# A hybrid decoder layer on one core: the RWKV part recast (inverse levels as an engine loop, chunk steps as a scan, group norm in two token parts)

## The reference, cut to what matters

```python
def step(s, inp):                      # s: (N, H, E_value, E_key)
    r_t, w_t, k_t, v_t, a_t, b_t = inp
    sa = jnp.einsum('nhvk,nhk->nhv', s, a_t)
    s = s * w_t[:, :, None, :] + sa[..., None] * b_t[:, :, None, :] + v_t[..., None] * k_t[:, :, None, :]
    return s, jnp.einsum('nhvk,nhk->nhv', s, r_t)
...
mu_y = jnp.mean(y, axis=-1, keepdims=True)
var_y = jnp.mean(jnp.square(y - mu_y), axis=-1, keepdims=True)
y = ((y - mu_y) * lax.rsqrt(var_y + RWKV_GN_EPS)).reshape(n, t, RWKV_W)
y = y * lp['rwkv_ln_w'] + lp['rwkv_ln_b']
y_rwkv = ((y + bonus.reshape(n, t, RWKV_W)) * g).astype(h.dtype)
```

## Time and profile before

| what | value |
|---|---|
| median of 3 runs | 2193.56 us (2188.53 to 2202.67) |
| profiled execution, its own time | 2205.53 us |
| its span in the profile | 2203.7 us |
| granted PE clock, mean | 0.975 |
| PE / DVE / ACT / POOL busy | 97% / 54% / 39% / 9% |

### The profile page before, as it was taken

The page is one execution under the profiler, slowest core; times in us unless marked ns, Lnnn a source line. Parts: engine busy times, 40 slices in busy tenths (PEclk is TensorE's granted clock), DMA queues, the critical chain, the costliest instruction groups (busy, mean ns, idle before and its releaser), DMA issues.

```text
span 2203.7 us, 46115 instructions
## 1 busy us (share of the span) xinstructions
PE 2126.8 (97%) x19116; PEld 2095.9 (95%) x19116; DVE 1191.8 (54%) x1232; ACT 857.5 (39%) x954; POOL 194.6 (9%) x158
## 2 busy tenths in 40 slices
PE   6999999999999999999987889999999999999997
PEld 5999999999999999999985779999999999999997
DVE  5555555555455454769766446555555555544442
ACT  4444444444344343443323114444444444433332
POOL 3000000000000010044104720100000000000000
PEclk9999999999999999999997859999999999999998
DMA  5555555555555556587850105655555555555552
GB/s 158 183 180 182 180 181 181 181 180 182 172 182 188 174 186 189 163 224 230 255 160 9 32 24 175 188 180 180 178 185 179 183 179 181 182 165 194 189 170 97
DMA packets 359032, 373.52 MB, mean 169 GB/s; under 512 B 13329, under 2 KB 351797, under 8 KB 358742
## 3 DMA queue, kind: packets, MB, share of 16 engines
q1 hardware_dynamic: 349280, 348.17, 49.7%
q0 software_dynamic: 5920, 17.48, 3.1%
q10 hardware_dynamic: 3742, 6.52, 0.9%
HBM read 366.82 MB, written 5.32 MB: 169 GB/s over the span
## 4 chain that ended last, share of the span: by engine, by line
PE 91%; DVE 5%; DMA 2%; ACT 1%; issue 1%; ACTq 0%; POOL 0%; SPq 0%; POOLq 0%; DVEq 0%
PE ps L305 28%; PE ps L307 28%; PE ps L306 28%; DMA raw<-in_w_in_dram 2%; DVE wL L292 1%; PE ps L1066 1%; PE ps L1394 1%; PE ps L1609 1%; PE ps L1582 1%; PE ps L1678 0%; DVE xL L339 0%; PE ps L1601 0%; ACT wH L286 0%; PE ps L1665 0%; PE ps L1760 0%
## 5 line engine op out<-in xcount | busy, mean ns | idle before, releaser
L292 DVE TENSOR_TENSOR wL<-raw,wH 128x1024 fp32r<-128x1024 f32 (+1 forms) x676 | 828.4, 1231 | 864.1 <-ACT wH L286 863.8
L286 ACT ACTIVATE wH<-raw 128x1024 fp32r<-128x1024 f32 (+1 forms) x676 | 699.9, 1037 | 1013.5 <-PE ps L307 948.2
L305 PE MATMUL ps<-xH,wH 128*128 128x264 f32 x3616 | 1031.8, 285 | 12.6 <-DVE wL L292 12.6
L307 PE MATMUL ps<-xH,wL 128*128 128x264 f32 x3616 | 1029.7, 285 | 0.0
L306 PE MATMUL ps<-xL,wH 128*128 128x264 f32 x3616 | 1029.5, 285 | 0.0
L305 PEld LDWEIGHTS ps<-xH,wH 128*128 128x128 f32 x3616 | 683.9, 189 | 14.6 <-issue 13.9
L307 PEld LDWEIGHTS ps<-xH,wL 128*128 128x128 f32 x3616 | 683.5, 189 | 0.0
L306 PEld LDWEIGHTS ps<-xL,wH 128*128 128x128 f32 x3616 | 683.0, 189 | 0.2
L305 PE MATMUL ps<-hH,wH 128*128 128x264 f32 x1408 | 402.4, 286 | 0.0
L307 PE MATMUL ps<-hH,wL 128*128 128x264 f32 x1408 | 401.4, 285 | 0.0
L306 PE MATMUL ps<-hL,wH 128*128 128x264 f32 x1408 | 401.3, 285 | 0.0
(11 more groups left out here) (331 smaller groups left out, 1219.2 us busy)
## 6 DMA issues: line engine op xcount, KB each, us to landing
raw<-in_ffn_w_gate_dram SPq DMA_DIRECT2D x176, 512.0 KB, 3.4
raw<-in_ffn_w_up_dram SPq DMA_DIRECT2D x176, 512.0 KB, 3.5
raw<-in_ffn_w_down_dram SPq DMA_DIRECT2D x128, 512.0 KB, 3.5
raw<-in_w_in_dram SPq DMA_DIRECT2D x100, 512.0 KB, 4.8
raw<-in_ffn_w_down_dram SPq DMA_DIRECT2D x64, 384.0 KB, 3.1
raw<-in_w_out_dram SPq DMA_DIRECT2D x32, 512.0 KB, 4.6
kb<-in_cache_swa_k_dram POOLq DMA_DIRECT2D x24, 256.0 KB, 6.5
vb<-in_cache_swa_v_dram ACTq DMA_DIRECT2D x24, 256.0 KB, 5.4
```

Source lines behind the costliest of these rows:

```text
L286: nc.scalar.activation(wH[:, k % RING, 0:nk, :], raw[:, k % RING, 0:nk, :], ACT.Copy).then_inc(S("head_made"), 1)
L292: nc.vector.tensor_tensor(wL[:, k % RING, 0:nk, :], raw[:, k % RING, 0:nk, :], wH[:, k % RING, 0:nk, :].bitcast(F32), ALU.subtract).then_i ...
L305: nc.tensor.matmul(out, wH[:, k % RING, q, cols], high, start=a, stop=False)
L307: last = nc.tensor.matmul(out, wL[:, k % RING, q, cols], high, start=False, stop=b)
```

## The change

- The five levels are an engine loop on PE (`pe.Fori`), with waits against a register. The other engines' lists stay unrolled. Z's layout changes so that two heads of one pair lie side by side, and X is no longer grown: at each level PE transposes Z (six 128x128 transposes a pair) and ACT copies the result to `Xq`. The grams of X are gone; Aak comes ahead of the levels, the reads (Arb, Ark) behind them.
- The chunk steps become a scan: U is solved for all chunks at once (`pe_solved`, with own values and turned aT as one 128-column right side), a transition matrix is made for chunks 1 to 3 (`pe_transition`), and the state goes from chunk to chunk by one product and one DVE operation (`pe_state`, `state`). Outputs come in two groups (`pe_outputs`). Keys are turned for both the b and the k operand at once (`pe_turn_keys`).
- Group norm has two token parts (0 to 127, 128 to 263). The gain is multiplied into the spreading matrix `hs` by GpSimd during the gates (with a table `lnwr` loaded for it), the bias is added to `bv` by ACT; the gating runs on DVE for both parts.
- Samples: GpSimd first makes the products for S.a and then for S.(w r), the output is put together from them and two dot products, and then the state is updated and written. ACT's four heads of the output projection stand behind both RWKV heads; DVE's four tails stand at its end.

The diff, cut to its core:

```diff
+        with pe.Fori(0, LEVELS) as lv:
+            for n in range(2):
+                pe.wait_ge(S("grams_out"), 2 * n + 2)
+                pe.wait_ge(S("z_level"), lv * 2 + (n + 1))
+                for i in range(RT):
+                    pair = Zq[n][:, 2 * i:2 * i + 2, :].rearrange("p b c -> p (b c)")
+                    last = nc.tensor.transpose(wide(slice(0, P), 4 + 2 * n, i), pair, ident)
+                last.then_inc(S("level_x"), 1)
+                for i, b, cp in every():
+                    last = nc.tensor.matmul(place(HALF[b], 2 * n + cp, i), Aq[n][HALF[cp], slot(b, i), :],
+                                            Zq[n][HALF[cp], 2 * i + b, :], start=True, stop=True)
+                last.then_inc(S("level_q"), 1)
+            for n in range(2):
+                pe.wait_ge(S("grams_out"), 4)
+                pe.wait_ge(S("level_q_out"), lv * 2 + (n + 1))
+                pe.wait_ge(S("level_x_out"), lv * 2 + (n + 1))
+                for i, b, cp in every():
+                    last = nc.tensor.matmul(place(HALF[cp], 2 * n + b, i), Xq[n][HALF[b], i, cp, :],
+                                            Qq[n][HALF[b], slot(cp, i), :], start=True, stop=True)
+                last.then_inc(S("level_z"), 1)
...
+    def pe_solved(pe, m, first):
+
         for i, b, cp in every():
+            R = HALF[cp]
+            rhs = side_by_side(R, FQ_AT[m] * H + slot(b, i), TOKA_AT[m] * H + 2 * i + b)
+            last = nc.tensor.matmul(wide(HALF[1 - cp], first, 2 * i + b), Zq[m][R, 2 * i + b, :], rhs,
+                                    start=True, stop=True)
+        last.then_inc(S("solved"), 1)
...
+    def pe_state(pe, n, bank):
+
+        for i, b in both():
+            h, out = 2 * i + b, place(HALF[b], bank, i)
+            last = nc.tensor.matmul(out, KB[n][:, h, :], UV[n][:, h, :], start=True, stop=n == 0)
+            if n:
+                last = nc.tensor.matmul(out, LR[HALF[b], n - 1, i, C:2 * C], states[n - 1][HALF[b], i, :],
+                                        start=False, stop=True)
+        last.then_inc(S("states_made"), 1)
...
     def pe_chunks(pe):
         pe_inverse(pe)
+        pe_own_values(pe, 0, 4)
+        pe_own_values(pe, 1, 6)
+        pe.wait_ge(S("z_level"), 11)
+        pe_reads(pe, 1, 0)
+        pe.wait_ge(S("z_level"), 12)
+        pe_turn_keys(pe, 1, 2)
+        pe.wait_ge(S("tokens_staged"), 8)
+        pe_solved(pe, 0, 4)
+        pe.wait_ge(S("tokens_staged"), 9)
+        pe_turn_keys(pe, 0, 2)
+        pe.wait_ge(S("grams_out"), 5)
+        pe.wait_ge(S("tokens_staged"), 10)
+        pe_solved(pe, 1, 0)
+        pe.wait_ge(S("solved_v"), 3)
+        pe.wait_ge(S("solved_a"), 3)
+        pe_transition(pe, 1, 4)
+        pe_state(pe, 0, 7)
...
```

DVE's new list behind the levels, where the place of the sample reduce is to be seen:

```diff
+        reads(0)
+        solved(0)
+        solved(1)
+        transition(1)
+        state(1)
+        dve.wait_ge(S("sample_parts"), 3)
+        v.tensor_reduce(smy[:], S2[:, :, 0:C // 2], AX.X, ALU.add).then_inc(S("sample_sums"), 1)
+        reads(1)
+        state(2)
```

GpSimd's new list:

```diff
+        step(g.tensor_tensor(S2[:], S1[:], key(0), ALU.mult))
+        halve()
+        g.tensor_tensor(ycat[:], sv[:, 2:4, :], sv[:, 4:5, :].broadcast_to([96, 2, C]), ALU.mult
+                        ).then_inc(S("sample_parts"), 1)
+        step(g.tensor_tensor(sv[:, 0, :], sv[:, 1, :], sv[:, 4, :], ALU.mult))
+        pool.wait_ge(S("sample_sums"), 1)
         step(g.tensor_tensor(S2[:], S1[:], key(0), ALU.mult))
         halve()
         step(g.tensor_tensor(S1[:], S1[:], key(1), ALU.mult))
-        pool.wait_ge(S("sample_sums"), 1)
+        pool.wait_ge(S("sample_sums"), 3)
+        for value, dot in ((smal[:, 0:C], smal[:, C:C + 1]), (sv[:, 5, :], smal[:, C + 1:C + 2])):
+            step(g.tensor_scalar(ycat[:, 0, :], value, dot, None, ALU.mult))
+            step(g.tensor_tensor(smy[:], smy[:], ycat[:, 0, :], ALU.add))
+        for a in range(2):
+            g.tensor_scalar(ycat[:, a, :], smy[:], cgat[:, 48 + a:49 + a], None, ALU.mult).then_inc(S("sample_y"), 1)
         step(g.tensor_tensor(S2[:], val(smal[:, 0:C]), key(2), ALU.mult))
         step(g.tensor_tensor(S1[:], S1[:], S2[:], ALU.add))
         step(g.tensor_tensor(S2[:], val(sv[:, 5, :]), key(3), ALU.mult))
         g.tensor_tensor(S1[:], S1[:], S2[:], ALU.add).then_inc(S("sample_state"), 1)
         pool.wait_ge(S("sample_state"), 1)
         pool.dma_start(o[9][0].rearrange("b h v k -> (b h) v k"), S1[:]).then_inc(S("sample_state_out"), 16)
-        step(g.tensor_tensor(S2[:], S1[:], key(4), ALU.mult))
-        halve()
         pool.wait_ge(S("sample_state_out"), 16)
```

More of the change, by code:

```diff
@@ L1527, in build @@
     HALF = (slice(0, C), slice(C, P))
[L1528 to L1535, removed]
+    ORDER = (1, 2, 3, 0)
     def mask(m, bits=False):
@@ new lines, in pe_turn_keys, with pe_reads @@
+    def pe_turn_keys(pe, n, first):
+        c = chunk(n)
+        for i in range(RT):
+            low, high = (bT, pkr) if n % 2 else (pkr, bT)
+            nc.tensor.transpose(wide(HALF[0], first, i), low[:, i, c], ident)
+            last = nc.tensor.matmul(wide(HALF[1], first, i), high[:, i, c], ident, start=True, stop=True)
+        last.then_inc(S("tokens_turned"), 1)
+    def pe_reads(pe, n, first):
+        c = chunk(n)
+        for i in range(RT):
+            for k in range(4):
+                b, own = k % 2, k // 2 ^ k % 2
+                last = nc.tensor.matmul(place(HALF[n % 2 if own else 1 - n % 2], first + b, i),
+                                        (pkr if own else bT)[HALF[b], i, c], pr[HALF[b], i, c], start=True, stop=True)
+        last.then_inc(S("grams_made"), 1)
@@ new lines, in pe_outputs @@
+    def pe_outputs(pe, m, first):
+        for n in (2 * m, 2 * m + 1):
+            for i, b in both():
+                h, k = 2 * i + b, i % 3 * P + n % 2 * C
+                out = ps[HALF[b], first + i // 3, k:k + C]
+                last = nc.tensor.matmul(out, UV[n][:, h, :], AR[n][:, slot(b, i), :], start=True, stop=n == 0)
+                if n:
+                    last = nc.tensor.matmul(out, states[n - 1][HALF[b], i, :], LR[HALF[b], n - 1, i, 0:C],
+                                            start=False, stop=True)
+        last.then_inc(S("outputs"), 1)
@@ new lines, in solved @@
+        def solved(m):
+            first = (6, 2)[m]
+            act.wait_ge(S("solved"), m + 1)
+            cp(threes(Wq[m][:, RT:H]), wide_half(slice(0, P), first, 2, 1), ACT.Copy).then_inc(S("solved_a"), 1)
+            for q in range(2):
+                R = HALF[1 - q]
+                cp(threes(UV[2 * m + q][:, RT:H], R), wide_half(R, first, 2, 0), ACT.Copy).then_inc(S("solved_a"), 1)
+        keys(0)
+        keys(1)
+        solved(0)
+        solved(1)
+        keys(2)
+        keys(3)
@@ new lines, in solved, with transition @@
+        def solved(m):
+            first = (4, 0)[m]
+            dve.wait_ge(S("solved"), m + 1)
+            v.tensor_copy(threes(Wq[m][:, 0:RT]), wide_half(slice(0, P), first, 2, 1)).then_inc(S("solved_v"), 1)
+            for q in range(2):
+                R = HALF[1 - q]
+                v.tensor_copy(threes(UV[2 * m + q][:, 0:RT], R), wide_half(R, first, 2, 0)).then_inc(S("solved_v"), 1)
+        def transition(n):
+            first = (4, 0, 4)[n - 1]
+            out = LR[:, n - 1].rearrange("p (g i) (w c) -> p g i w c", g=2, w=2)
+            dve.wait_ge(S("transitions"), n)
+            eye = cm[:, 0:1, :].unsqueeze(1).broadcast_to([P, 2, 3, C])
+            linked([v.tensor_tensor(out[:, :, :, 1, :], wide_half(slice(0, P), first, 2, 1), eye, ALU.add)], dve)
+            v.tensor_tensor(out[:, :, :, 0, :], wide_half(slice(0, P), first, 2, 0),
+                            pr[:, :, chunk(n)].rearrange("p (g i) c -> p g i c", g=2), ALU.add
+                            ).then_inc(S("transitions_out"), 1)
@@ L1958, in dve_chunks @@
+        reads(1)
+        state(2)
+        reads(2)
+        transition(2)
+        reads(3)
+        state(3)
+        transition(3)
+        dve_group_centre(dve, 0)
+        state(4)
         dve.wait_ge(S("sample_turned_y"), 1)
         v.tensor_copy(pvr[:, :, T:N].rearrange("p j b -> p b j"),
-                      ps[:, 6, 384:432].rearrange("p (b j) -> p b j", b=NB)).then_inc(S("sample_y_placed"), 1)
-        dve_group_centre(dve, 2)
-        for k in range(2):
-            tail(dve, CK, OUT, OUT_PER, 0, k)
```

532 lines of the change are left out of this document (208 added, 324 removed).

## The result

The changed kernel takes 2228.7 us (median of four runs, 2223.7 to 2230.4), the kernel before 2191.6 beside it: a ratio of 1.0156 [1.0116, 1.0196]. It is slower by 1.6%, where 2163 and "faster" were forecast, and the time lies above the range. The profiled execution took 2230.4 us, 24.9 more than that of before; the medians differ by 37, since the profiled execution of before was 12 above its median.

A forecast was written before the change was run, and what follows sets the result against it. TensorE matmuls bound the feed-forward blocks and projections, left alone; each changed stretch had another limit. The first pair's output products were to reach 1303.0 instead of 1333.3, 30.3 us off the median 2193.56, forecasting 2163 us, range 2150 to 2196.

The forecast's parts named there:

- Start: Grams before the levels: fewer operands awaited, last own gram finished about 1199.6 where the first level began 1199.8, gain 0.2.
- Levels: Five inverse levels: 5.0 us an iteration, plus 1.4 for first-pass code; PE leaves at 1225.7, not 1247.9, gain 22.
- Loop refetched: Rival: the levels' loop code is fetched every iteration, 11.1 us instead of 5.0, time 2194 or 2220; chance 0.09.
- Chunk steps: From the levels' end at 1225.7 through solving, state scan, outputs and sums, at full clock, ending at 1259.6.
- Two more 1.4: PE in the chunk steps: two more state products after the first state's 0.7 us, at 1.4 us each.
- so I take 1.0: Chunk steps: PE clock taken as full, because nearly all products now use both row halves.
- Tile shapes alternate: Rival: in states and outputs K=128 and K=64 pairs alternate, 0.17 for each of 144 switches, time 2178; chance 0.13.
- Clock falls: Rival: PE clock drops in the chunk steps, their 29.5 us of PE work doubles, gain 4, time 2189; chance 0.22.
- Turned keys: PE in the chunk steps: 18 records of 128 columns, 1.5 us a call at full clock.
- Group norm: Two-part group norm and gating behind the chunk steps: 20.6 us, to 1280.2, against 29.6 before.
- Sample part on GpSimd: GpSimd waits 9 us for DVE's reduce; its state write lands at 1287 and is last, first output product 1289.4.
- The anchor: Gain worked out from the profiled execution of 2205.5 us, 12 above the median, but taken off the median 2193.56.

The follow-up runs named there:

- x2: Changed kernel with each group's twelve 128-row own products first, then twelve 64-row carried ones, sum of the two left out: 2178.9 us, one run.
- x1: Changed kernel in the same order, but carried state and output products overwrite the own ones instead of adding to them: 2224.5 us, one run.
- x4: Changed kernel with own and carried products alternating two by two, sum of the two left out: 2185.6 us, one run.
- the quadrant versions: Changed kernel with each 128-row state and output product split into two 64-row ones in two banks, added by DVE; first such version 2181.2 us, ratio 0.9948.
- e7: Changed kernel with the turned keys' transposes made plain products with the identity, order kept: 2217.9 us, one run.
- q5: The first of the quadrant versions, with DVE's reduce of the samples' output sum moved up behind the first reads: 2177.1 us, ratio 0.9925.
- e4: Changed kernel with the turned keys grouped, six transposes and then six products, instead of alternating: 2218.6 us, ratio 1.0113.

## Why the prediction was wrong

*Start and Levels* held: the loop starts at 1199.2 for 1199.6. Its first iteration took 7.2 us because the clock was at 0.50 in it up to 1203.3, the others 5.4 for 5.0 (the last 5.1), PE left at 1227.8 for 1225.7. PE's first four groups of an iteration took 3.2 us for 2.9, and from there to the next turn it was 2.25 for 2.07. The 1.4 for code in the first pass hardly came: in x2, where the clock stood at 1.0, that pass took 5.6 (1198.19 to 1203.83). The rival *Loop refetched* falls: q8 has fewer packets, and no iteration waits for code. By the Trainium skill (Runtime: NRT & Kernel Launch, Instruction fetch mechanics) a taken branch out of the current window forces a fetch; here neither the packets nor the gaps show one for a loop of 408 instructions, and it was the unrolled form that waited for code.

*Chunk steps* is the step that failed, in two of its terms. "Two more 1.4" (1.4 each, by the sum of 19.8) and "outputs 4.9" priced the changes of shape at nothing, and "so I take 1.0" gave them the full clock. Measured: states 1 to 3 took 7.8, 9.6 and 7.7 us and the outputs 30.3. The price itself stood in the rival *Tile shapes alternate*: 0.17 for each of 144 switches. At the full clock it was right: x2 runs four records in 0.138 us (22 own in 0.89, 22 carried in 0.64), the changed kernel in 0.514, so 0.19 a change. Too low was its chance, and a row behind it was misread. The 0.15 after L1646 had been taken as a cost of one way only, since "the way back shows nothing lost". The trace of before shows the way back too: six L1414 records start at 1250.19, 0.109 apart, and L1678 comes 0.20 behind the last of them, 0.09 late, and so it does behind the last L1414 at 1244.83.

```profile
1250.94 1.61 PE L1678 MATMUL ps<-Fc,Zq 64*64 64x64 f32 x24
```

So both ways cost, and in a group where each product changes, every product pays. The Trainium skill (TensorEngine Tiling (Array Packing), Key Properties) says that changing the tiling mode drains the engine, without a number; x1 to x4 fit that and give a price, and no run shows the draining itself.

The two rivals were also priced as if only one could come true. *Clock falls* (2189) and *shapes* (2178) each fit the range; both came, and one brought the other. In x2, x4 and the quadrant versions the chunk steps keep 1.00; where every product changes shape, the granted clock drops to 0.50 at 1254.5, three microseconds into state 1. What each adds can be estimated: 144 products at 0.257 and chunk 0's twelve at 0.08 are 38.0 us, and x2's are 10.9, so 27 for the changes at the full clock; measured are 55.4, so 17 more for the half clock. Together 44.5. From the start of state 0 to ACT's `mixH` the changed kernel takes 95.0 us and x2 40.5; the ten left of that difference are the half clock on what lies between (the turned keys, 5.85 us a call for 3.55, the transitions, the sums). In the time 49.8 are left, mainly because x2 then waits 5.6 for the state's write.

*Turned keys* "1.5 each" were 3.55, a change of kind that no rival had. That e7 takes 1.5 is luck: the forecast had 18 records one after the other, e7 has 24, two side by side.

*Group norm* held in form: in q5, from the end of the first sums (1268.8) to the weight tail's end (1290.0) are 21.2 us for 20.6.

*Sample part on GpSimd* held too, with its end hidden: the wait was 13.4 for 9 and the write would have landed at 1293.3 for 1287, because DVE's reduce ended at 1250.7 for 1244.7: 2.1 of that came from the levels, 4.1 from two calls of turned keys. In x2 it is what ends last, with the first product at 1293.1 for the 1289.4 of the sum. So without the alternation the sum's 30.3 us would have been 26.6 by the profiled times (2205.5 - 2178.9).

*The anchor* failed as well. The gain was worked out from one execution of before and taken off the median, 12 us below it. The runs of before on record follow their mean granted clock: the seven at 0.974 to 0.976 took 2199.2 to 2208.2 us, those at 0.983 and above took 2185.8 to 2194.5, and the profiled one had 0.975. Between 1190 and 1362 its trace has 67 us at the half clock; outside that stretch all traces of this case have 38 to 50, and behind the fourth chunk of the output projection all have the same 870.2 to 870.4. So the 12 us lie most likely in the very stretch that the change replaces, and were counted twice; only one trace of before was kept, so this is inferred. By the profiled times the forecast is 2175.2. x2's 2178.9 is 16 above 2163: 3.7 from the sample part, 12 from this.

The signs listed were the right ones: "PEclk 0.50 in the chunk steps" and "state products above 2 us" both came.

## What to carry to other kernels

Before merging products of other shapes, or transposes, into one accumulation order, count how often neighbours on PE differ, and price each change at 0.2 us until a row says otherwise; then ask what the granted clock does meanwhile, since the two multiply. Run by shape, or cut all products to one shape: the quadrant version has half as many instructions again in states and outputs, and takes 47 us less. Two rivals with a common cause need a case of their own. And before a gain read from one trace is taken off a median, compare the granted clock of the profiled execution with that of the other runs.

## What was not expected of the hardware

- A run of one shape costs about 0.26 us from its start to the next one's at 2.4 GHz whether it holds two records or four, and 0.40 with two at 1.2 GHz; unchanged shapes go at 0.029 (64x64 pairs) and 0.040 (128x64) a record.
- The clock: with PE busy throughout in the records, it stood at 0.50 for 61 us (1254.5 to 1315.9) in the changed kernel's chunk steps, and at 1.00 where the same products were sorted by shape (x2).
- A transpose among plain products of its own shape costs too, 0.13 us a change (3.55 against 2.23 us for six pairs, ten changes fewer).
- Plain products on 128 rows and 64 columns took 0.12 us each with the two column halves in turn (e7) and 0.24 each on one half (e4), two records in both cases. A transpose, one record, took 0.13 in a row.
